# Three weight buffers of two tiles instead of two of three, in a two-block network kernel

## What is computed

```python
for l in range(DEPTH):                                   # DEPTH = 2
    h = rmsnorm(x, norm_w[l])
    proj = jnp.einsum("bsd,de->bse", h, w_in[l])         # 2048 -> 6160
    ... = jnp.split(proj, split_idx, axis=-1)
    y_ssd = ssd_branch(...)                              # conv, chunked state space scan
    y_cfm = conformer_branch(...)                        # gated conv of 31 taps
    y_att = diff_attention_branch(...)                   # 4 heads, two softmaxes each
    y = jnp.concatenate([y_ssd, y_cfm, y_att], axis=-1)
    x = x + jnp.einsum("bse,ed->bsd", y, w_out[l])       # 2048 -> 2048
```

## Time and profile before

| | |
|---|---|
| median of 3 runs | 3073.88 us (3073.58 to 3075.14) |
| the profiled execution | 3075.18 us, of which its span 3073.9 us |
| TensorE busy | 2975.6 us, 97% |
| VectorE, ScalarE, GpSimd busy | 1766.3, 974.4 and 2019.9 us |
| HBM read | 275.08 MB, 94 GB/s over the span |
| mean granted clock of TensorE | 0.991 |

### The profile page before, as it was taken

How to read it: one execution, slowest core, us unless ns; L and a number is a source line. 1 busy time by engine, 2 the same in 40 slices (tenths; PEclk the granted TensorE clock), 3 DMA queues, 4 the chain that set the end, 5 groups by cost and what they waited for, 6 DMA issues and landing times.

```text
span 3073.9 us, 39316 instructions
## 1 busy us (share of the span) xinstructions
PE 2975.6 (97%) x15124; PEld 2347.5 (76%) x15124; DVE 1766.3 (57%) x2344; ACT 974.4 (32%) x1683; POOL 2019.9 (66%) x1897
## 2 busy tenths in 40 slices
PE   8999999999999999999999899999999999899997
PEld 6887877788778878777887677777777777688886
DVE  8645887751474569776317433333778887910612
ACT  5343123320234331333103223223444444511411
POOL 7666676576676657755757655555676777567766
PEclk9999999999999999999999999999999999999999
DMA  4322222243223222222432222222222122142222
GB/s 156 124 98 95 96 89 79 80 142 128 102 100 110 103 78 94 91 81 76 174 123 98 76 80 72 84 72 80 71 77 81 69 83 83 56 158 96 98 95 96
DMA packets 56939, 295.51 MB, mean 96 GB/s; under 512 B 6544, under 2 KB 6928, under 8 KB 26928
## 3 DMA queue, kind: packets, MB, share of 16 engines
q1 hardware_dynamic: 37856, 253.77, 23.4%
q10 hardware_dynamic: 18896, 39.22, 3.8%
HBM read 275.08 MB, written 12.65 MB: 94 GB/s over the span
## 4 chain that ended last, share of the span: by engine, by line
PE 74%; DVE 15%; ACT 4%; POOL 3%; issue 2%; DMA 1%; ACTq 1%; DVEq 0%; SPq 0%; POOLq 0%
PE bank L439 60%; PE bank L963 6%; POOL w_lo L2619 2%; DVE rec_ex L2435 1%; DVE rec_cum L2300 1%; PE bank L773 1%; POOL w_hi L2617 1%; ACT att_sc L1321 1%; PE bank L782 1%; PE bank L790 1%; PE bank L955 1%; DMA w_raw<-in_wall 1%; DVE att_sc L2176 1%; DVE bank L1902 1%; DVE rec_lk L2427 1%
## 5 line engine op out<-in xcount | busy, mean ns | idle before, releaser
L439 PE MATMUL bank<-h_hi,w_lo 128*128 128x512 f32 x3456 | 1396.2, 404 | 30.9 <-POOL w_lo L2619 28.7
L2619 POOL TENSOR_TENSOR w_lo<-w_raw,w_hi 128x512 fp32r<-128x512 f32 x936 | 1306.6, 1396 | 78.0
L439 PE MATMUL bank<-h_hi,w_hi 128*128 128x512 f32 x3456 | 1354.8, 392 | 0.0
L439 PE MATMUL bank<-h_lo,w_hi 128*128 128x512 f32 x3456 | 1352.8, 391 | 0.0
L2617 POOL TENSOR_SCALAR w_hi<-w_raw 128x512 fp32r<-128x512 f32 x936 | 716.4, 765 | 964.8 <-PE bank L439 828.1
L439 PEld LDWEIGHTS bank<-h_hi,w_lo 128*128 128x128 f32 x3456 | 653.7, 189 | 225.0 <-issue 60.4
L439 PEld LDWEIGHTS bank<-h_hi,w_hi 128*128 128x128 f32 x3456 | 652.7, 189 | 140.7
L439 PEld LDWEIGHTS bank<-h_lo,w_hi 128*128 128x128 f32 x3456 | 654.3, 189 | 135.8 <-issue 8.4
L1024 ACT ACTIVATE raw<-bank 128x512 f32<-128x512 f32 x148 | 88.6, 599 | 406.3 <-PE bank L439 367.3
L2101 DVE SCALAR_TENSOR_TENSOR bank<-cfm_up,par,bank 128x512 f32<-128x512 f32 x232 | 175.4, 756 | 8.3
L2262 DVE TENSOR_TENSOR xT<-bank,xT 128x512 f32<-128x512 f32 x32 | 22.1, 692 | 218.1 <-PE bank L439 217.4
(11 more groups left out here) (376 smaller groups left out, 2977.9 us busy)
## 6 DMA issues: line engine op xcount, KB each, us to landing
w_raw<-in_wall SPq DMA_DIRECT2D x232, 1024.0 KB, 4.9
ssd_abc<-acs_scratch ACTq DMA_DIRECT2D x16, 512.0 KB, 3.7
x_scratch<-xT ACTq DMA_DIRECT2D x8, 1024.0 KB, 4.5
xT<-x_scratch ACTq DMA_DIRECT2D x8, 1024.0 KB, 8.9
xT<-in_x ACTq DMA_DIRECT2D x4, 1024.0 KB, 9.5
xT<-in_x SPq DMA_DIRECT2D x3, 1024.0 KB, 11.0
out<-last_z SPq DMA_DIRECT2D x4, 768.0 KB, 3.3
w_raw<-in_wall SPq DMA_DIRECT2D x8, 256.0 KB, 9.5
```

What stands on the lines that cost most here:

```text
L439: mm = t.matmul(bank[BANK[u]][:, :], w[:, CS16[k]], h[:, k, :], start=(k == 0 and w is m.w_lo[b]), stop=(k == KT - 1 and w is m.w_hi[b] an ...
L2619: g.tensor_tensor(m.w_lo[b][:, part], m.w_raw[b][:, part], m.w_hi[b][:, part].bitcast(F32), ALU.subtract).then_inc(*s.lo.inc(u, n))
```

## The change

Three buffers of two tiles take the room of two of three. `w_lo` of a buffer now lies at the same addresses as its `w_raw`: GpSimd's subtraction writes each element over the one that it has read. The buffer of unit u is `u % 3`. A load writes into a tile that TensorE reads, so SyncE starts the load of unit u when TensorE has read unit u-3 (`s.unit`); GpSimd waits for the landing alone. Five units, `QUARTERED` (the second and fourth of `FIRST`, but for the very first second one, which was loaded in pieces already), are loaded in four pieces, each when its quarter of unit u-3 has been read. GpSimd takes units strictly one after the other, except for units 0 and 1.

```diff
-PAIRS = [(names[n], names[n + 1]) for names in FIRST.values() for n in (0, 2)]
-PAIRS += [(("wo", l, KT - 2), ("wo", l, KT - 1)) for l in range(DEPTH)]
-PAIRED = frozenset(UNIT[pair[0]] for pair in PAIRS)
-OUT_PAIR = {UNIT["wo", l, 0]: l for l in range(DEPTH + 1)}
+NW = 3
+QUARTERED = frozenset(UNIT[names[n]] for names in FIRST.values() for n in (1, 3)) - {UNIT[FIRST[0][1]]}
...
-        self.w_raw = [big(f"w_raw{b}", [P, KT * P]) for b in range(2)]
-        self.w_hi = [big(f"w_hi{b}", [P, KT * P], F32R) for b in range(2)]
-        self.w_lo = [big(f"w_lo{b}", [P, KT * P], F32R) for b in range(2)]
+        self.w_hi = [big(f"w_hi{b}", [P, KT * P], F32R) for b in range(NW)]
+        raws = self.at
+        self.w_raw = [big(f"w_raw{b}", [P, KT * P]) for b in range(NW)]
+        self.at = raws
+        self.w_lo = [big(f"w_lo{b}", [P, KT * P], F32R) for b in range(NW)]
...
-    u = 2
-    while u < N_UNITS:
-        behind_pair = u - 2 in PAIRED or u - 2 in OUT_PAIR
-        us = (u, u + 1) if u in PAIRED or behind_pair else (u,)
-        for b in us:
-            g.wait_ge(*s.raw[b % 2].at(b))
+    for u in range(2, N_UNITS):
+        if u not in QUARTERED:
+            g.wait_ge(*s.raw[u % NW].at(u))
         for n in range(PIECES):
-            if behind_pair and n < PIECES - 1:
-                g.wait_ge(*s.pe.at("piece", u - 2, n))
-            elif u - 1 in OUT_PAIR and n < PIECES - 1:
-                g.wait_ge(*s.pe.at("read", OUT_PAIR[u - 1], n))
-            elif n == 0 or behind_pair or u - 1 in OUT_PAIR:
-                g.wait_ge(*s.unit.at(us[-1] - 2))
-            for b in us:
-                split(b, n)
-        u += len(us)
+            if u in QUARTERED:
+                g.wait_ge(*s.piece[1][n].at(u))
+            split(u, n)
...
     for u in range(2, N_UNITS):
-        b = u % 2
-        nc.sync.wait_ge(*s.lo.at(u - 2, PIECES - 1))
-        nc.sync.dma_start(m.w_raw[b][:, :], io["wall"][u, :, :]).then_inc(*s.raw[b].inc(u))
+        b = u % NW
+        if u in QUARTERED:
+            for n in range(PIECES):
+                at = slice(n * PIECE, (n + 1) * PIECE)
+                nc.sync.wait_ge(*(s.pe.at("piece", u - NW, n) if n < PIECES - 1 else s.unit.at(u - NW)))
+                nc.sync.dma_start(m.w_raw[b][:, at], io["wall"][u, :, at]).then_inc(*s.piece[1][n].inc(u))
+        else:
+            if u >= NW:
+                nc.sync.wait_ge(*s.unit.at(u - NW))
+            nc.sync.dma_start(m.w_raw[b][:, :], io["wall"][u, :, :]).then_inc(*s.raw[b].inc(u))
```

More of the change, by code:

```diff
@@ L100, in __init__ @@
         self.half = [signal(f"half{n}", 16) for n in "qk"]
-        self.raw = [signal(f"raw{b}", 16) for b in range(2)]
+        self.raw = [signal(f"raw{b}", 16) for b in range(NW)]
         self.con, self.con1, self.par, self.wd, self.pos, self.p = (signal(n, 16) for n in ("con", "con1", "par", "wd", "pos", "p"))
@@ L953, in product @@
                 at = slice((2 * (n % 2) + k) * T, (2 * (n % 2) + k) * T + T)
-                for h, w in ((q.phi, m.w_lo[u % 2]), (q.plo, m.w_hi[u % 2]), (q.phi, m.w_hi[u % 2])):
-                    mm = t.matmul(ps[:, :], h[:, k, CS[c]], w[:, at], start=(k == 0 and w is m.w_lo[u % 2]),
-                                  stop=(k == 1 and h is q.phi and w is m.w_hi[u % 2]))
+                for h, w in ((q.phi, m.w_lo[u % NW]), (q.plo, m.w_hi[u % NW]), (q.phi, m.w_hi[u % NW])):
+                    mm = t.matmul(ps[:, :], h[:, k, CS[c]], w[:, at], start=(k == 0 and w is m.w_lo[u % NW]),
+                                  stop=(k == 1 and h is q.phi and w is m.w_hi[u % NW]))
             mm.then_inc(*(s.unit.inc(u) if j % 8 == 7 else pe.inc("e", j)))
@@ L961, in gate_part @@
             at = slice(r * T, r * T + T)
-            for h, w in ((m.h_hi, m.w_lo[u % 2]), (m.h_lo, m.w_hi[u % 2]), (m.h_hi, m.w_hi[u % 2])):
-                mm = t.matmul(bank[GATE_BANK[c]][:, :], h[:, k, CS[c]], w[:, at], start=(k == 0 and w is m.w_lo[u % 2]),
-                              stop=(k == KT - 1 and h is m.h_hi and w is m.w_hi[u % 2]))
+            for h, w in ((m.h_hi, m.w_lo[u % NW]), (m.h_lo, m.w_hi[u % NW]), (m.h_hi, m.w_hi[u % NW])):
+                mm = t.matmul(bank[GATE_BANK[c]][:, :], h[:, k, CS[c]], w[:, at], start=(k == 0 and w is m.w_lo[u % NW]),
+                              stop=(k == KT - 1 and h is m.h_hi and w is m.w_hi[u % NW]))
             if c == NC - 1 and r == 3:
@@ L2615, in split @@
     def split(u, n):
-        b, part = u % 2, slice(n * PIECE, (n + 1) * PIECE)
+        b, part = u % NW, slice(n * PIECE, (n + 1) * PIECE)
         g.tensor_scalar(m.w_hi[b][:, part], m.w_raw[b][:, part], 1.0, 1.0, ALU.mult, ALU.mult).then_inc(*s.hi.inc(u, n))
@@ L2623, in pool_engine @@
         for u in range(2):
-            g.wait_ge(*s.piece[u][n].at("w"))
+            g.wait_ge(*s.piece[u][n].at(u))
             split(u, n)
-    u = 2
-    while u < N_UNITS:
-        behind_pair = u - 2 in PAIRED or u - 2 in OUT_PAIR
-        us = (u, u + 1) if u in PAIRED or behind_pair else (u,)
-        for b in us:
-            g.wait_ge(*s.raw[b % 2].at(b))
-        for n in range(PIECES):
-            if behind_pair and n < PIECES - 1:
-                g.wait_ge(*s.pe.at("piece", u - 2, n))
-            elif u - 1 in OUT_PAIR and n < PIECES - 1:
-                g.wait_ge(*s.pe.at("read", OUT_PAIR[u - 1], n))
-            elif n == 0 or behind_pair or u - 1 in OUT_PAIR:
-                g.wait_ge(*s.unit.at(us[-1] - 2))
-            for b in us:
-                split(b, n)
-        u += len(us)
+    for u in range(2, N_UNITS):
+        if u not in QUARTERED:
+            g.wait_ge(*s.raw[u % NW].at(u))
+        for n in range(PIECES):
+            if u in QUARTERED:
+                g.wait_ge(*s.piece[1][n].at(u))
+            split(u, n)
     q, n = m.last, NC - 1
@@ L2674, in pieces @@
             at = slice(n * PIECE, (n + 1) * PIECE)
-            nc.sync.dma_start(m.w_raw[u][:, at], io["wall"][u, :, at]).then_inc(*s.piece[u][n].inc("w"))
+            nc.sync.dma_start(m.w_raw[u][:, at], io["wall"][u, :, at]).then_inc(*s.piece[u][n].inc(u))
     x_part(0)
```

## The result

The change made the kernel slower. Its median is 3090.11 us (4 runs, 3088.57 to 3097.09) against 3074.51 us (4 runs, 3073.58 to 3076.29) before: ratio 1.0055, 95% interval 1.0039 to 1.0071. The forecast was 3054.0, its range 3043 to 3067. The profiled execution took 3088.7 us, its span 3087.4.

What follows compares the result with a forecast made beforehand. TensorE, busy 97% of the span, was taken as the bound, losing time at stage borders to waits for GpSimd. Terms -7.3 - 15 + 2.5 = -19.8 us gave a median of 3054.1 us, range 3043 to 3067.

Steps and rivals of the forecast that it cites:

- First output pair: First output product's last two units: TensorE's waits and lower clock go, the pair takes 21.8 us; -7.3 us.
- Second pair and the second block's start: Second output product's pair up to the scores: waits for GpSimd go, VectorE then bounds it; -15 us, the largest term.
- The split in place: GpSimd's subtraction over its own input takes as long as before, near 1.27 us; cost 0.
- The loads in quarters: The five units loaded in four pieces: landing takes between 4.9 and 9.5 us, soon enough at the tightest place.
- Rivals 4 and 5: GpSimd bounds through slower subtraction, 3215 us (within 0.05); loads stuck on SyncE's stream, 3067 us (0.20 together with Rival 1).
- signs of being wrong: `w_lo` median above 1.4 us; steady-stretch GpSimd waits; second block's L472 not 13 to 14 us earlier; attention's waits changed over a us.
- First layers' starts: Both blocks' first layer: no gain, waits for ScalarE grow, a lower clock behind them costs +1.5 and +1.0 us.
- Where the engines meet: VectorE and GpSimd slow each other; moved splits shift TensorE's waits by 0.9 us up or down; no term in the sum.
- In a steady stretch ... Cost nothing: Load started after TensorE reads unit u-3: first piece ready after 6.8 us, wanted after 21.8, 15 us spare; cost nothing.
- Rival 1: Second block: splits slow four `h_lo` by 0.9 us each, both clock drops cost 3.9; -11, 3063 us; 0.20 with rival 5.
- slower: Whole kernel slower, by GpSimd becoming the bound (3215 us) or by a sum of shifted waits (no size given); chance 0.05.
- a rival in which it brought a gain: First layer's start: GpSimd idle under VectorE's long `h_lo`, waits in attention and recurrence shrink; -28, 3046 us; chance 0.10.

Runs made afterwards that it cites:

- e1: Changed kernel, but except at stage borders GpSimd splits unit u only after TensorE has read unit u-2; 3057.14 us, 0.9948 of the kernel before.
- e2: Changed kernel, but only in the recurrence's 40 units GpSimd waits for TensorE to have read unit u-2; 3072.32 us, 0.9999 of the kernel before.
- e4: Changed kernel, but in the recurrence the split of the next head's `hf` (six units) waits for VectorE's scans to end; 3064.84 us, 0.9974 of the kernel before.
- e6: Changed kernel with e1's waits outside the recurrence and e4's wait in it; 3051.11 us, 0.9927 of the kernel before.
- e8: e1, but the six `hf` splits behind the heads' scans are let go as in the changed kernel; 3063.16 us, 0.9965 of the kernel before.
- e7: Kernel before, two buffers of three tiles, with an output product's last two units split one after the other; 3059.92 us, 0.9954 of the kernel before.

## Why the prediction was wrong

**What was right.** The bound at the borders and the sizes there. First output pair: -7.3 forecast, from 7.4 to 0.6 in the table, -6.8. Second pair and the second block's start: -15 forecast, from 6.0 to -10.4, -16.4 (e1: -14.9), with the forecast wait for `h_lo` L1820 of 2 to 4 us (2.66); the 1.6 us for a lower clock behind it did not come (1.00 over the 12 us that follow). The split in place: 0, as forecast. The loads in quarters: 3.6 us, below both bounds that I gave. Waits for GpSimd: the start's alone, as forecast. Rivals 4 and 5 did not come. Two of my signs of being wrong did: L472 of the second block came 0.6 us earlier and not 13 to 14, and attention's wait for `att_sm` L2176 grew from 1.4 us in all to 7.5.

**First layers' starts: right in kind, too small.** I took +1.5 and +1.0. The first is +3.2: the wait grew to 6.32 us, and the granted clock in 95 to 110 us is 0.77, where it was 1.00. The second is +0.7 from 835.5 to 924.1 (0.6 to 1.3).

**The step that failed** is "Where the engines meet": "I give that no term in the sum". I had the rows that a split and a VectorE instruction slow each other, and wrote of shifts of 0.9 us up or down, as if they cancelled. They don't, for two reasons that rows of before bear on:

- The kernel before had GpSimd's splits released by TensorE, and VectorE's chain hangs on TensorE's products too, through ScalarE, so the two stood in the same phase head by head (the chain is 29.3 us in five heads on end). The change lets the landing release the splits, and so a new phase repeats as many times (32.0 to 32.2 us in four of the same heads, 33.4 in one). It cost +4.2 us from 109 to 645, +4.7 from 924 to 1460, and +24 in the recurrence, of which I had none. The executions of e2 and e4, with the same code there, lose 5.6 and 5.4 us in the first of these stretches, and from 835 to 1460 both 7.4, where the changed kernel's profiled one loses 5.4.
- There was no slack: TensorE waited 0.41 us for `rec_lk` before, so the chain bounded each head. A shift towards less overlap could win little more than that wait (e6: 66.99 us a head against 67.65), one towards more costs all that the chain grows by, 3 to 7 us with the clock. The bet is lopsided.

"In a steady stretch ... Cost nothing" was argued for the load, which is right, and silently taken for the split as well. Rival 1 had the mechanism, but in one place (four `h_lo`) and at 3063 us; my "slower", "a sum of shifted waits", had 0.05 and no price. The sum that fits the profiled execution is -6.8 - 16.4 + 3.2 + 0.7 + 4.2 + 4.7 + 24 = +13.6, the table's last row.

That a VectorE instruction and a split slow each other is shown by e6, e8 and e4: the same scans at 3.64, 5.76 and 8.30 us by nothing but the split's place. The Trainium skill, SBUF — State Buffer, section "SBUF: two separate sides", states that the two engines share a port which one instruction holds while it runs. The trace agrees in direction, but not with a holder that keeps the other out: a split (7.6 us alone) and eight scans (3.64 alone) would take 11.3 us one after the other, and took 8.32 together. I cited that section, priced a loss by it at 1.3 us each time, and then used it only for a rival in which it brought a gain.

**What stays open.** How a head's loss in the changed kernel parts between the chain and the lower clock is read from its trace alone, by the heads at 1.00 and at 0.98; why the clock fell in some heads and not in others, behind the same waits, stays open. That the splits between the borders cost the 4.2 and 4.7 us is shown by e1 (0.1 and 1.0 us gained there), not which of VectorE's instructions; the waits for `att_sm` grew most. A kernel with the recurrence's splits left out wasn't tried.

## What to carry to other kernels

When a change alters what releases a helper engine's work, it alters the work's phase against every other engine, in each repetition. List for the bound's critical chain what slack it has (here none: TensorE already waited 0.4 us a head for it) and which helper instructions lie beside it now and would then. An extra buffer lets work run early; whether early is good has to be decided place by place: here a third buffer with free-running splits lost 16 us, and the same buffer with splits held where they were, and six of them behind a scan, won 22. And try the small part alone: one condition, which splits two units one by one, gave 13.5 us with the two buffers as they were.

## What the runs showed of the hardware

- A scan of 128 x 128 on VectorE takes 0.45 us with GpSimd idle (3.64 for 8, e6) and 1.04 under a split (8.32 for 8): 2.3 times as long. Multiplications of 128 x 512 take 0.69 us with GpSimd idle (e8) and 0.9 or 1.6 beside a split, 1.3 or 2.3 times. The split under the scans is hardly slowed: its subtractions stay at 1.29 us and its copies take 0.73 instead of 0.62, where beside VectorE's multiplications they take 1.6 and 1.06. So who pays depends on the kind of instruction.
- TensorE ran a head at a clock of 1.00 with a wait of 1.44 us in it (e8), and at 0.95 with 3.08 and one more of 1.03. With waits of 2.2 and 0.7 us it ran two heads of the changed kernel at 1.00 and two at 0.98. After 3.2 us of waits at the first output pair it ran at 0.72 over 12 us, after 1.51 at 1.00 (e7).
